# Sample attention with value groups between key groups, and a reordered front, in a hybrid decoder step

## The reference

```python
def decoder_layer(x, pos, attend, s0, ffn1, mix, ffn2):
    x = x + 0.5 * swiglu(rms_norm(x, ffn1[0]), ffn1[1], ffn1[2], ffn1[3])
    y, k, v, ik, s_new = mixer_block(rms_norm(x, mix[0]), pos, attend, s0, *mix[1:])
    x = x + y
    x = x + 0.5 * swiglu(rms_norm(x, ffn2[0]), ffn2[1], ffn2[2], ffn2[3])

# indexed_sparse_attention, for each of 8 sequences of the sample:
    dots = jnp.einsum('bthd,bsd->bths', iq, ik_all)          # 4 index heads over 2056 positions
    score = jnp.einsum('bths,bth->bts', jax.nn.relu(dots), iw * IDX_W_SCALE)
    _, idx = lax.top_k(score, n_sel)                         # 256 positions kept
    logits = jnp.einsum('bthd,btkhd->bthk', q, k_sel) * (HEAD_DIM_A ** -0.5)
    p = jax.nn.softmax(logits, axis=-1)
    return jnp.einsum('bthk,btkhd->bthd', p, v_sel)          # 8 heads of 64
```

## Time and profile before

| | |
|---|---|
| time, median of 3 runs | 1862.19 us (1859.61 to 1864.7) |
| the profiled execution | 1853.4 us, span 1851.4 us |
| PE busy | 1673.8 us, 90% |
| DVE, ACT, POOL busy | 776.6, 452.3, 629.0 us (42%, 24%, 34%) |
| mean DMA rate | 110 GB/s, 203.57 MB |
| mean granted TensorE clock | 0.946 |

### The profile page before, as it was taken

The page is one execution under the profiler, slowest core; times in us unless marked ns, Lnnn a source line. Parts: engine busy times, 40 slices in busy tenths (PEclk is TensorE's granted clock), DMA queues, the critical chain, the costliest instruction groups (busy, mean ns, idle before and its releaser), DMA issues.

```text
span 1851.4 us, 28848 instructions
## 1 busy us (share of the span) xinstructions
PE 1673.8 (90%) x12749; PEld 1540.3 (83%) x12753; DVE 776.6 (42%) x1185; ACT 452.3 (24%) x633; POOL 629.0 (34%) x286
## 2 busy tenths in 40 slices
PE   6999999999977999676999987785799999999998
PEld 5999999999757999564887754454799999999998
DVE  6423012254253798576756342231655223012231
ACT  4221112123441234001233332230223221112111
POOL 2433344443211345742142432322232433343332
PEclk9999999999998999888999997986899999999999
DMA  5232334334201223111322277877422232333222
GB/s 158 79 92 63 86 106 111 85 106 137 78 24 49 82 82 92 46 49 42 134 72 75 74 266 293 298 292 258 193 69 81 80 92 63 86 92 92 62 79 83
DMA packets 193501, 203.57 MB, mean 110 GB/s; under 512 B 6225, under 2 KB 179345, under 8 KB 184929
## 3 DMA queue, kind: packets, MB, share of 16 engines
q1 hardware_dynamic: 173040, 105.56, 20.0%
q0 software_dynamic: 12832, 80.29, 12.0%
q10 hardware_dynamic: 7504, 15.88, 2.3%
HBM read 187.21 MB, written 14.30 MB: 109 GB/s over the span
## 4 chain that ended last, share of the span: by engine, by line
PE 80%; DVE 9%; DMA 5%; issue 3%; ACT 2%; POOL 1%; ACTq 0%; SPq 0%; DVEq 0%; POOLq 0%
PE ps L1513 22%; PE ps L1515 21%; PE ps L1514 21%; PE ps L1943 3%; DMA v_page<-in_cache_v,kv_row 2%; DMA k_page<-in_cache_k,kv_row 2%; PE ps L1960 1%; PE ps L2021 1%; PE ps L1894 1%; DVE m_hi L1459 1%; PE ps L1912 1%; PE ps L1903 1%; DVE k_lev L1261 1%; DVE att L1241 1%; PE ps L1526 1%
## 5 line engine op out<-in xcount | busy, mean ns | idle before, releaser
L469 POOL TENSOR_TENSOR w_lo<-raw,w_hi 128x2048 fp32r<-128x2048 f32 (+2 forms) x108 | 456.7, 4228 | 931.2 <-ACT w_hi L603 931.2
L1513 PE MATMUL ps<-n_lo,w_hi 128*128 128x288 f32 x1824 | 545.2, 299 | 1.0 <-ACT qT L711 1.0
L1514 PE MATMUL ps<-n_hi,w_lo 128*128 128x288 f32 x1824 | 539.8, 296 | 0.0
L1515 PE MATMUL ps<-n_hi,w_hi 128*128 128x288 f32 x1824 | 538.0, 295 | 0.0
L1513 PEld LDWEIGHTS ps<-n_lo,w_hi 128*128 128x128 f32 x1824 | 343.5, 188 | 15.9 <-issue 15.1
L1515 PEld LDWEIGHTS ps<-n_hi,w_hi 128*128 128x128 f32 x1824 | 345.2, 189 | 0.0
L1514 PEld LDWEIGHTS ps<-n_hi,w_lo 128*128 128x128 f32 x1824 | 344.2, 189 | 0.1
L603 ACT ACTIVATE w_hi<-raw 128x2048 fp32r<-128x2048 f32 (+2 forms) x108 | 187.7, 1738 | 274.6 <-PE ps L1515 273.8
L1513 PE MATMUL ps<-hid_lo,w_hi 128*128 128x288 f32 x704 | 208.8, 297 | 0.0
L1514 PE MATMUL ps<-hid_hi,w_lo 128*128 128x288 f32 x704 | 207.7, 295 | 0.0
L1515 PE MATMUL ps<-hid_hi,w_hi 128*128 128x288 f32 x704 | 207.0, 294 | 0.0
(11 more groups left out here) (296 smaller groups left out, 2389.2 us busy)
## 6 DMA issues: line engine op xcount, KB each, us to landing
raw<-in_ffn_w_gate SPq DMA_DIRECT2D x44, 512.0 KB, 4.0
raw<-in_ffn_w_up SPq DMA_DIRECT2D x44, 512.0 KB, 5.2
raw<-in_ffn_w_down SPq DMA_DIRECT2D x32, 704.0 KB, 4.7
raw<-in_w_in SPq DMA_DIRECT2D x22, 1024.0 KB, 5.3
scratch_g<-g_out POOLq DMA_DIRECT2D x8, 576.0 KB, 3.2
gates<-scratch_g ACTq DMA_DIRECT2D x4, 1152.0 KB, 8.9
raw<-in_w_out SPq DMA_DIRECT2D x4, 1024.0 KB, 5.3
scratch_x<-xT ACTq DMA_DIRECT2D x1, 2304.0 KB, 11.9
```

The lines of the kernel that those rows point to most:

```text
L469: pool.tensor_tensor(w_lo[:, u % NRAW, :n], raw[:, u % NRAW, :n], w_hi[:, u % NW, :n].bitcast(F32), ALU.subtract).then_inc(S("w_lo_done"), 1)
L1513: pe.matmul(dst, hi, x_lo, start=first, stop=False)
L1514: pe.matmul(dst, lo, x_hi, start=False, stop=False)
L1515: return pe.matmul(dst, hi, x_hi, start=False, stop=last)
```

## The change

Sample attention: TensorE still does pair 0's keys alone. From pair 1 on, the turns of the probabilities of pair p - 1 stand around the first dots of pair p, and the value groups of pair p - 1 are put, in halves, between the turns of the key groups of pair p; the last two (`LEFT`) follow after the pair's last dots. POOL issues the loads in that order, and waits for all gate stores before the fourth key group. Turns use two PSUM banks, 4 and 5. The key group that begins a pair is turned ahead of the last dots of the pair before it.

Front: `lows` subtracts in pieces of 512 columns and the gate product is done in two pieces; ScalarE splits the unit after next as soon as a unit is done, ahead of the copies that follow (`split(u + 2)`), and copies out turned tiles before it takes the square root of the norm; the norm of the first feed-forward is in a new `second_unit`; `kept_s` is one copy by VectorE in place of two more copies of each tile by ScalarE and VectorE, and the ReLU of the new index dots stands ahead of the score copies; the load of `v_new` is issued within prompt attention.

```diff
-        KP_BANK = (4, 5, 7)
+        KP_BANK = (4, 5)
+        LEFT = 2
@@ POOL, lows
-                    pool.tensor_tensor(w_lo[:, u % NRAW, :n], raw[:, u % NRAW, :n], w_hi[:, u % NW, :n].bitcast(F32),
-                                       ALU.subtract).then_inc(S("w_lo_done"), 1)
+                    for at in range(0, n, 512):
+                        part = slice(at, min(at + 512, n))
+                        ins = pool.tensor_tensor(w_lo[:, u % NRAW, part], raw[:, u % NRAW, part],
+                                                 w_hi[:, u % NW, part].bitcast(F32), ALU.subtract)
+                    ins.then_inc(S("w_lo_done"), 1)
@@ POOL, attention_pages
-                    pool.tensor_tensor(part, part, rms[:, :].unsqueeze(1).to_broadcast([P, 2, T]),
-                                       ALU.mult).then_inc(S("gate_scaled"), 1)
+                    for a in range(2):
+                        ins = pool.tensor_tensor(part[:, a, :], part[:, a, :], rms[:, :], ALU.mult)
+                    ins.then_inc(S("gate_scaled"), 1)
...
-                for m in range(K_RING, 8):
-                    key_group(m)
                 for m in range(2):
                     pool.wait_ge(S(f"gate_stored{m}"), 64)
-                for pair in range(4):
-                    if pair < 3:
-                        for n in range(8):
-                            key_group(8 * pair + 8 + n)
-                    for n in range(8):
-                        value_group(8 * pair + n)
+                for m in range(K_RING, 2 * K_RING):
+                    key_group(m)
+                    value_group(m - K_RING)
+                for m in range(2 * K_RING, 9):
+                    key_group(m)
+                for pair in range(1, 4):
+                    for n in range(LEFT if pair > 1 else 0):
+                        value_group(8 * pair - 8 - LEFT + n)
+                    key_group(8 * pair + 1)
+                    for n in range(1, 8):
+                        if 8 * pair + n + 1 < 32:
+                            key_group(8 * pair + n + 1)
+                        m = 8 * pair - 8 + n - 1
+                        if n <= 8 - LEFT and m >= V_RING:
+                            value_group(m)
+                for m in range(24 - LEFT, 32):
+                    value_group(m)
@@ ACT, token_major
-                    split(u + 1)
                     act.wait_ge(S("unit_done"), u + 1)
...
                     ins.then_inc(S("stage_done"), 1)
+                    split(u + 2)
                     if i == 2:
                         index()
-                    if OK_ == TOKEN_COLS[i][0] // 512 * 512 or OQ == TOKEN_COLS[i][0] // 512 * 512:
+                    if i != 2:
+                        turn_out(i - 1)
+                    if i in NORMED:
                         act.wait_ge(S("qk_ss"), NORMED.index(i) + 1)
...
-                    if i != 2:
-                        turn_out(i - 1)
@@ ACT, index
+                        if ph == 3:
+                            act.wait_ge(S("new_dots"), 1)
+                            act.activation(rel[:, 0, 0:2 * NS], ps[:, 1, 0:2 * NS], ACT.Relu).then_inc(S("rel_new"), 1)
                         for e in range(2):
-                            for dst in (score_s, kept_s):
...
@@ ACT, the start
+            split(1)
             for c in range(DC):
                 squared(0, c)
-                if c == 4:
-                    split(1)
+            split(2)
@@ DVE, index
                 dve.wait_ge(S("scored"), 4)
+                link(dve.tensor_copy(kept_s[:, :], score_s[:, :]))
@@ PE, first_unit and the unit after it
-                        elif k == DC - 1:
-                            norm(0)
...
+            def second_unit(hi, lo):
+
+                norm(0)
+                for m in (1, 0):
+                    if m == 0:
+                        pe.wait_ge(S("rms_done"), 1)
+                    for k in range(DC):
...
@@ PE, sample_attention
+                for hp in range(4):
+                    turn(hp)
+                for n in range(8):
+                    for hp in range(4):
+                        turn(4 * n + 4 + hp)
+                    dots(0, n)
+                new_dots(0)
                 for pair in range(1, 4):
-                    keys(pair)
-                    values(pair - 1)
+                    if pair >= 2:
+                        for n in range(8 - LEFT, 8):
+                            values(pair - 2, n, (0, 1, 2, 3))
+                    prob_turn(pair - 1, 0)
+                    prob_turn(pair - 1, 1)
+                    dots(pair, 0)
+                    for j in range(2, 5):
+                        prob_turn(pair - 1, j)
+                    pe.wait_ge(S("spT_done"), 5 * pair)
+                    for hp in range(4):
+                        turn(32 * pair + 4 + hp)
+                    new_values(pair - 1)
+                    for n in range(1, 8):
+                        for half in range(2):
+                            if 8 * pair + n + 1 < 32:
+                                for hp in range(2 * half, 2 * half + 2):
+                                    turn(32 * pair + 4 * n + 4 + hp)
+                            if n <= 8 - LEFT:
+                                values(pair - 1, n - 1, (2 * half, 2 * half + 1))
+                        dots(pair, n)
+                        if n == 3 and pair >= 2:
+                            rows_turn(pair - 2)
+                    new_dots(pair)
+                for n in range(8 - LEFT, 8):
+                    values(2, n, (0, 1, 2, 3))
+                for j in range(5):
+                    prob_turn(3, j)
+                new_values(3)
                 rows_turn(2)
-                values(3)
+                for n in range(8):
+                    values(3, n, (0, 1, 2, 3))
                 rows_turn(3)
```

More of the change, by code:

```diff
@@ L768, in features @@
                 ins.then_inc(S("stage_done"), 1)
+                split(at_unit["tok", i] + 2)
                 def shaped(r):
@@ L855, in prompt_attention @@
                         gate_out(n - 1)
+                    if n == 4 * HA - 1:
+                        act.wait_ge(S("pp_dots"), 4 * HA)
+                        act.dma_start(v_new[:, :], out[7][0].rearrange("b q h d -> (b q) (h d)")).then_inc(S("v_new_back"), 16)
                     if n == 18:
@@ L864, in sample_attention, with keys @@
             def sample_attention():
-                act.wait_ge(S("pp_dots"), 4 * HA)
-                act.dma_start(v_new[:, :], out[7][0].rearrange("b q h d -> (b q) (h d)")).then_inc(S("v_new_back"), 16)
-                def keys(pair):
-                    for n in range(0, 32, 2):
-                        m = 32 * pair + n
+                def keys(g):
+                    for m in range(4 * g, 4 * g + 4, 2):
                         act.wait_ge(S("kp_turned"), m + 1)
@@ L895, in turned @@
                         ins.then_inc(S("spT_done"), 1)
-                keys(0)
-                probabilities(0)
+                for g in range(9):
+                    keys(g)
                 for pair in range(1, 4):
-                    keys(pair)
+                    probabilities(pair - 1)
                     turned(pair - 1)
-                    probabilities(pair)
+                    for g in range(8 * pair + 1, min(8 * pair + 9, 32)):
+                        keys(g)
+                probabilities(3)
                 turned(3)
@@ L1558, in first_unit @@
                                                 start=turn == 0 and k == 0, stop=turn == 2 and k == DC - 1)
+                ins.then_inc(S("unit_done"), 1)
+            def second_unit(hi, lo):
[4 more added lines that the diff above has]
+                    for k in range(DC):
+                        at = (m * DC + k) * P
+                        for t in range(2):
+                            ins = product(ps[:, 4 + 2 * m + t, 0:HT], hi[:, at:at + P], lo[:, at:at + P],
+                                          n_hi[:, k, t * HT:(t + 1) * HT], n_lo[:, k, t * HT:(t + 1) * HT],
+                                          k == 0, k == DC - 1)
                 ins.then_inc(S("unit_done"), 1)
@@ L1974, in new_dots @@
                     ins.then_inc(S("sp_dots"), 1)
-                def keys(pair):
-                    for n in range(8):
-                        if n == 0:
-                            for hp in range(4):
-                                if pair >= 2 and (32 * pair + hp) % 3 == 2:
-                                    pe.wait_ge(S("o_rows_done"), pair - 1)
-                                turn(32 * pair + hp)
-                            if pair >= 2:
-                                rows_turn(pair - 2)
-                        if n < 7:
-                            for hp in range(4):
-                                turn(32 * pair + 4 * n + 4 + hp)
-                        dots(pair, n)
-                    new_dots(pair)
                 def rows_turn(pair):
@@ L2015, in values @@
```

(14 more changed lines are left out.)

106 lines of the change are left out of this document (51 added, 55 removed).

## The result

The changed kernel takes 1809.78 us (median of 4 runs, 1808.42 to 1819.23) against 1861.12 us of the kernel before on the same chip (4 runs, 1859.61 to 1864.7): ratio 0.9732, 95% interval 0.9696 to 0.9769, faster by 51 us where 33.6 was forecast. The two profiled executions stand 45.0 us apart, 1853.4 and 1808.42: the profile of before lay 7.7 us under its median, that of after 1.4.

A forecast was written before the change was run, and what follows sets the result against it. Feed-forward was taken as bound by TensorE (100% busy), sample attention by page transfers with too few in flight. Gains 6.5 + 1.6 + 7.7 + 1.6 + 16.2 = 33.6 us off the 1862.2 median gave 1828.6 us, range 1813 to 1848.

The forecast's parts named there:

- Index part: Token-major stage: ReLU moved ahead of four score copies by ScalarE saves 3.9 us, less 0.4 for a split.
- Heads and prompt attention: From the first `left` of the recurrent heads to the last value product of prompt attention: forecast gain 0.
- m_lo: Last projections: rounding in pieces shortens TensorE's four waits for this buffer, 6.9 us; gain 6.5 us (bounds 4 and 6.9).
- Sample attention: New load schedule, priced at 2.83 us a page group: last rows at 1275.4 against 1291.6, gain 16.2 us (bounds -40 and 24).
- From here the queue stays fed: Sample attention: after some 8 us empty at the first pair boundary, 20 us of transfers cover TensorE's later pauses of about 16.
- K3 about 4 us late: Start of sample attention: the fourth key group's load issues at about 1073.1, not 1068.9; 4.2 us lost.
- Token-major: Token-major stage: ScalarE's new order shortens kT waits and lengthens the qT wait; 7.7 us with the index work (bounds 4 and 10).
- First norm: First feed-forward: norm done after unit 0 still starts near 39.7, unit 1 follows sooner; gain 1.6 us (bounds 0 and 4).
- Start of the heads: Recurrent heads: last split ahead of the SiLUs makes POOL ready for w_lo earlier; gain 1.6 us (bounds 0 and 2.5).
- D: Rival, sample attention: TensorE waits every round, falls to 1.2 GHz, 7.2 us a round for 24 rounds; 1882 us, chance 0.06.
- A: Rival: sample attention gains little, from a longer first boundary or POOL's single order starving each round; 1846 us, chance 0.2.
- C: Rival: no attention loss to clock or starts, bounds nearly reached elsewhere; 24 + 20 = 44 us, 1818 us, chance 0.15.

The follow-up runs named there:

- the two orders of loads that were tried: Changed kernel with key groups 3 to 5 loaded ahead of the gate-store wait: 1806.55 us; changed kernel with value group ahead of key group from each pair's third step: 1810.43 us.

## Why the prediction was right or wrong

The direction held; the size did not. By the means of the traces the stretches add up to some 48 us gained, by ratio it is 50, and 33.6 were forecast.

- **Index part, the step that failed.** "it now comes first: 3.9 us" counted one of the two places where ScalarE makes four copies. The other had a pause of 1.9 us of its own, visible in before's trace, that I did not list; and I priced neither pause with the clock behind it. Forecast 3.5, measured 8.6 in this pair of traces, 11.2 in the mean of all: the largest miss.
- **Heads and prompt attention, a term put at nothing.** For the pieces the prediction spoke of `m_lo` and of 0.9 us for each unit, and gave the heads and the prompt attention 0. By the means they gained 5.6 us there, with nearly the same idle time and a higher granted clock (0.904 for 0.890).
- **m_lo, a term mis-sized.** "gain 6.5 us (bounds 4 and 6.9)": the waits did vanish entirely, and the stretch gave 9.5 (pieces alone) to 10.5, in the mean 8.6. The upper bound was the sum of the waits; a bound must also hold what the clock gives back. `m_hi` at 1.45 us and `m_lo` at 1.73 are as predicted. The Trainium skill (SBUF, State Buffer, "Who interferes with whom") has the lock held for the whole instruction by whoever issues first; the 4.74 and 1.45 agree, and so does the alternation with single pieces.
- **Sample attention, two errors that cancelled, by luck.** The price of 2.83 us at 371 GB/s: 2.49 at 423, worth 0.34 us on each of 38 loads, 13 us. "From here the queue stays fed": the share was 0.72, 0.86 and 0.84 in the three periods, 12.9, 6.7 and 6.9 us short of full, of which only some 8 at the first boundary were allowed for. The step forgot that POOL issues in order and waits on a key slot that only the turns behind the softmax free. From the load of K3 to the last rows the sum gives 202.3 us (1275.4 less 1073.1), and it took 205.2. The first two periods, 46 and 48 us, are as forecast (47) for other reasons. The Trainium skill has both figures of the rate (DMA: Bandwidth & Descriptors, "Measured"): 341 GB/s for 1 MB by itself, 425 for 16 MB. The runs agree with the second when the queue is full (421 to 424 GB/s). As an estimate by that figure of the page, a load would have cost 2.47 us.
- **K3 about 4 us late**: 3.6, right. **Token-major** 4.2 for the three units, measured 6.3, half as much again. The waits for `kT` fell to 3.7 us each where 5 was forecast; those for `qT` rose by 1.8, as forecast. With the index part it is 14.9 us, above the bound of 10. **First norm** 1.6, measured 2.6 to 2.9. **Start of the heads** 1.6, measured 1.1.
- **The base.** I took gains between profiles off a median. That median and the profiled time of before differed by 7.7 us, of after by 1.4: 6.3 of the 17.7 us miss. Before ranges from 1843 to 1866 over some 80 executions, after from 1806 to 1819 over nine. The first trace of before had drawn fast cases in the index stretch (58.6 us, mean 61.9) and in heads and prompt attention (300.2, mean 305.9), which is why the gains read from it alone come out smaller there than the means.
- **Rivals.** D did not happen: the granted clock is 1.00 in the rounds and 0.72 to 0.94 in ten microseconds at each of three boundaries (0.56 at the last, from 1230 to 1240). A saw rightly that POOL's single order leaves the queue short, at the boundaries though and not in each round, and the faster loads paid for it. C was the nearest in size (44 us; 45.0 between the profiles), by other terms: it had 24 us from the attention, which gave 14.0.

Not settled: why the clock falls behind the 1.9 us pause in some executions and not in others, why it stands higher in the heads with the pieces, whether the front is more than its parts, and why three groups left gained 9.2 us.

## What to carry to other kernels

Price a short idle of TensorE as its length plus what the clock costs behind it, and look at each recurrence of a pattern (four copies, twice), not only at the one in the list's longest wait. Read the price of a transfer from a stretch in which the queue was full throughout, and ask at each phase boundary which slot the next load in order waits for. If one phase must stand still for a softmax, leave it work that has its data already: one more group left was worth more here (9.2 us in the trace) than the two orders of loads that were tried (3 and 0). And where a kernel's executions differ by more than the terms in question, compare a stretch over all traces that share its code, not one pair.

## What was not expected of the hardware

- VectorE and POOL alternate piece by piece when both have work: four pieces take 5.0 us alone, 5.9 beside `m_hi` and `m_lo`, and two units' eight pieces 13.6 us beside `n_lo`. The eight `n_lo` take 1.76 us each where they took 1.27 in the mean.
- Page loads reach 421 to 424 GB/s on one core, from one tensor or two.
- Behind one and the same pause of 1.9 us, in the same kernel code, TensorE ran on at 2.4 GHz in one execution and at 1.2 GHz for some 17 us in another: four matmuls of 1.93 us together took 3.67. In a third the 1.2 GHz lasted some 7 us. It makes 7 us of difference between executions of one kernel, a part of its spread.
